# First attention of a two-block transformer kernel: the value projection spread over two query blocks, and a pair's outputs copied out of their bank by ScalarE

## The reference, cut to what matters

```python
SEQ, QBLK, ATT_HEADS, ATT_HEAD_DIM = 512, 128, 16, 64
def forgetting_attention(q, k, v, log_f):
    scale = ATT_HEAD_DIM ** -0.5
    F = jnp.transpose(jnp.cumsum(log_f, axis=1), (0, 2, 1))
    q, k, v = (jnp.transpose(t, (0, 2, 1, 3)) for t in (q, k, v))
    for blk in range(S // QBLK):
        s0, s1 = blk * QBLK, (blk + 1) * QBLK
        logits = jnp.einsum('bhqd,bhkd->bhqk', q[:, :, s0:s1], k[:, :, :s1]) * scale
        logits = logits + F[:, :, s0:s1, None] - F[:, :, None, :s1]
        mask = jnp.arange(s0, s1)[:, None] >= jnp.arange(s1)[None, :]
        p = jax.nn.softmax(jnp.where(mask, logits, -jnp.inf), axis=-1)
        outs.append(jnp.einsum('bhqk,bhkd->bhqd', p, v[:, :, :s1]))
# q, k, v are columns of h @ w_in (h: 512 x 1024); all in float32
# beside it, independent of it: silu(c_2) @ mod_mix_w_2 and silu(c_2) @ mod_ffn_w_2
```

## Time and profile before

| what | us |
|---|---|
| median of three runs | 2661.47 |
| lowest and highest run | 2659.76, 2664.95 |
| span of the profiled execution, first to last instruction | 2654.8 |
| the attention stage in it, first matmul of the stage to the first of the next | 52.2 to 307.7 |
| one pair in it (pairs 1 to 5) | 30.0 |

### The profile page before, as it was taken

One profiled execution on the slowest core, in us unless ns is written; L12 is line 12 of the kernel. 1 busy time (PEld: TensorE's weight loads), 2 busy tenths in 40 slices (PEclk: granted clock), 3 DMA queues, 4 the chain that ended last, 5 costly groups with the idle time before them and its releaser, 6 DMA issues. The chain is left out here.

```text
span 2654.8 us, 33834 instructions
## 1 busy us (share of the span) xinstructions
PE 2503.1 (94%) x13321; PEld 1989.2 (75%) x13321; DVE 1729.9 (65%) x2508; ACT 1139.0 (43%) x1641; POOL 63.4 (2%) x166
## 2 busy tenths in 40 slices
PE   7999899999989999899988899999999989999998
PEld 5666578777767877788875457888888877788886
DVE  4899545588875666899965565677766664632435
ACT  5444422255564235688853344522324253531323
POOL 0000000000000001000001000000000000000000
PEclk9999999999999988999999999999999899999999
DMA  7887727333235734999962203234332423233321
GB/s 263 264 284 270 245 82 276 91 104 95 80 104 191 257 61 167 355 420 419 417 250 92 78 27 104 80 119 135 111 111 77 127 87 121 65 107 98 95 80 32
DMA packets 299502, 427.44 MB, mean 161 GB/s; under 512 B 27690, under 2 KB 213533, under 8 KB 289488
## 3 DMA queue, kind: packets, MB, share of 16 engines
q1 hardware_dynamic: 289424, 395.13, 43.4%
q0 software_dynamic: 5392, 20.97, 2.0%
q10 hardware_dynamic: 4528, 9.18, 0.9%
HBM read 384.11 MB, written 41.14 MB: 160 GB/s over the span
## 5 line engine op out<-in xcount | busy, mean ns | idle before, releaser
L3724 PE MATMUL banks<-big,late_parts 128*128 128x512 f32 x1920 | 443.0, 393 | 5.9 <-PEq L151 3.8
L3724 PEld LDWEIGHTS banks<-big,late_parts 128*128 128x128 f32 x1920 | 363.3, 189 | 84.1 <-issue 6.1
L3724 PE MATMUL banks<-h_parts_second,late_parts 128*128 128x512 f32 x1440 | 331.1, 390 | 4.7 <-DVE h_parts_second L3936 4.7
L3724 PEld LDWEIGHTS banks<-h_parts_second,late_parts 128*128 128x128 f32 x1440 | 271.0, 188 | 61.2 <-issue 5.1
L3912 DVE TENSOR_TENSOR late_parts<-w_second,late_parts 128x2048 fp32r<-128x2048 f32 x69 | 158.1, 2292 | 218.7 <-ACT late_parts L3797 218.5
L2379 DVE TENSOR_TENSOR expert_parts<-w,expert_parts 128x2048 fp32r<-128x2048 f32 x102 | 232.7, 2288 | 21.7 <-ACT expert_parts L2375 20.8
L3797 ACT ACTIVATE late_parts<-w_second 128x2048 fp32r<-128x2048 f32 x69 | 132.0, 1914 | 255.9 <-PE banks L3724 255.9
L1344 PE MATMUL banks<-h_parts,ssm_parts 128*128 128x512 f32 x960 | 229.0, 396 | 0.8 <-DVE ssm_parts L1611 0.4
L2375 ACT ACTIVATE expert_parts<-w 128x2048 fp32r<-128x2048 f32 x102 | 194.8, 1916 | 60.6 <-PE banks L2386 54.7
L1344 PEld LDWEIGHTS banks<-h_parts,ssm_parts 128*128 128x128 f32 x960 | 178.5, 188 | 43.3 <-issue 6.4
L2386 PE MATMUL banks<-expert_parts,expert_xt 128*128 128x512 f32 x816 | 192.4, 395 | 4.0 <-DVE expert_xt L2367 4.0
(11 more groups left out here) (703 smaller groups left out, 3851.2 us busy)
## 6 DMA issues: line engine op xcount, KB each, us to landing
w_second<-in_mlp_w_dram SPq DMA_DIRECT2D x64, 1024.0 KB, 5.2
w<-in_w_exp_gate_dram SPq DMA_DIRECT2D x34, 1024.0 KB, 9.6
w<-in_w_exp_up_dram SPq DMA_DIRECT2D x34, 1024.0 KB, 9.4
w<-in_w_exp_down_dram SPq DMA_DIRECT2D x34, 1024.0 KB, 9.2
w<-in_w_in_dram SPq DMA_DIRECT2D x64, 512.0 KB, 4.6
w<-in_mod_mix_w_dram SPq DMA_DIRECT2D x24, 1024.0 KB, 5.1
w<-in_mod_ffn_w_dram SPq DMA_DIRECT2D x23, 1024.0 KB, 5.9
w<-in_w_in_dram SPq DMA_DIRECT2D x16, 1024.0 KB, 5.7
```

Source lines behind the costliest of these rows:

```text
L3724: mm = pe.matmul(ps[:, bank(n, f), :], w_part(n, w)[:, kk, f * P:(f + 1) * P], x[:, v, kk, :], start=(first_chunk(n) and kk == 0 and j == ...
```

## The change

1. Value projection. A table `PIECES` gives the pieces of each block: query in block 0 and key in block 1 as before (12 + 12 matmuls), value in four pieces of 6, two in block 2 and two in block 3.
2. `turn_values(i)` moves from block 3 of the pair before to block 0 of the pair itself, ahead of the query projection, and writes the upper halves of banks 4 and 5, not bank 7. `turn(i, 0)` now waits for its copy, `v_copied`. `copy_values(i)` on ACT stands behind `exponent(i, 1)`.
3. `sum_mod(i-1)`, `copy_rows` and `turn_mod(i-1)` move from block 0 to block 1, and the wait for `mod_copied` and `copy_mod` from block 1 to block 2, since the values now use these half banks in block 0.
4. `copy_out(i-1)` moves from DVE to ACT, behind `copy_values(i)` in block 0; for the last pair it is ACT's last instruction.
5. `evict` and `high` of the value go from block 2 to block 3 on ACT; `low(i+2, 2)` on DVE goes from block 3 of pair i to block 0 of pair i+1 (there called `low(i+1, 2)`).
6. On SP `halves.load(0)`, which waits for the last `low`, goes from ahead of the first strip of pair 6 to ahead of its fourth.

```diff
@@ -790,2 +790,3 @@
     GROUP = 32
+    PIECES = (((0, 0, 4), (0, 4, 8)), ((1, 0, 4), (1, 4, 8)), ((2, 0, 2), (2, 2, 4)), ((2, 4, 6), (2, 6, 8)))
     mod_matrices = (k.ins["mod_mix_w_2"], k.ins["mod_ffn_w_2"])
@@ -853,3 +854,3 @@
                         load_qkv(k, sp, i + 2)
-                    if i == final - 1 and j == 0:
+                    if i == final - 1 and j == MOD_SLOTS:
                         sp.wait_ge(s["w_low"], 3 * pairs)
@@ -874,5 +875,3 @@
                     pe.wait_ge(s["w_low"], 3 * i + j + 1)
-                    if i > 0 and j == 0:
-                        pe.wait_ge(s["v_copied"], i)
-                    elif i > 0:
+                    if i > 0:
                         pe.wait_ge(s["proj_copied"], 3 * i + j)
@@ -887,4 +886,7 @@
                 pe.wait_ge(s["proj_copied"], 3 * i + 3)
+                if i > 0:
+                    pe.wait_ge(s["turned_copied"], UNITS * i)
                 for b in range(TB):
-                    mm = pe.transpose(ps[:, 7, b * P:(b + 1) * P], vt[:, b * P:(b + 1) * P], k.ident[:])
+                    at = HALF + b % 2 * P
+                    mm = pe.transpose(ps[:, 4 + b // 2, at:at + P], vt[:, b * P:(b + 1) * P], k.ident[:])
                 mm.then_inc(s["v_turned"], 1)
@@ -905,4 +907,5 @@
             def turn(i, b):
-                if b == 0 and i > 0:
-                    pe.wait_ge(s["turned_copied"], UNITS * i)
+                if b == 0:
+                    pe.wait_ge(s["v_copied"], i + 1)
+                if b == 1 and i > 0:
                     sum_mod(i - 1)
@@ -918,6 +921,4 @@
             def weigh(i, b):
-                if b == 0:
-                    pe.wait_ge(s["v_copied"], i + 1)
-                    if i > 0:
-                        pe.wait_ge(s["o_copied"], i)
+                if b == 0 and i > 0:
+                    pe.wait_ge(s["o_copied"], i)
                 pe.wait_ge(s["turned_copied"], UNITS * i + 2 * b + 2)
@@ -962,3 +963,2 @@
             project(0, 2, 0, KD)
-            turn_values(0)
             pe.wait_ge(s["mask_ready"], 2)
@@ -971,8 +971,7 @@
                         scores(i + 1, 0)
+                    if b == 0:
+                        turn_values(i)
                     if i + 1 < pairs:
-                        if b < 3:
-                            project(i + 1, b, 0, KD // 2)
-                        else:
-                            turn_values(i + 1)
-                    if i > 0 and b == 1:
+                        project(i + 1, *PIECES[b][0])
+                    if i > 0 and b == 2:
                         pe.wait_ge(s["mod_copied"], i)
@@ -983,4 +982,4 @@
                     turn(i, b)
-                    if i + 1 < pairs and b < 3:
-                        project(i + 1, b, KD // 2, KD)
+                    if i + 1 < pairs:
+                        project(i + 1, *PIECES[b][1])
                     if i == final and 1 <= b < 3:
@@ -988,3 +987,3 @@
                     weigh(i, b)
-                    if i > 0 and b == 0:
+                    if i > 0 and b == 1:
                         turn_mod(i - 1)
@@ -1009,3 +1008,4 @@
                 act.wait_ge(s["v_turned"], i + 1)
-                act.activation(v[:, i % 2], ps[:, 7, :].rearrange("p (b n) -> p b n", b=TB), ACT.Copy).then_inc(s["v_copied"], 1)
+                dst = v[:, i % 2].rearrange("p (e b) n -> p e (b n)", e=2)
+                act.activation(dst, ps[:, 4:6, HALF:], ACT.Copy).then_inc(s["v_copied"], 1)
 
@@ -1043,2 +1043,6 @@
                 ins.then_inc(s["mod_copied"], 1)
+
+            def copy_out(i):
+                act.wait_ge(s["weighed"], duals * (i + 1))
+                act.activation(o[:, i, :], ps[:, 6, :], ACT.Copy).then_inc(s["o_copied"], 1)
 
@@ -1059,3 +1063,2 @@
                 high(1, j)
-            copy_values(0)
             exponent(0, 0)
@@ -1067,12 +1070,15 @@
                         exponent(i + 1, 0)
-                        copy_values(i + 1)
-                    if i > 0 and b == 1:
+                    if b == 0:
+                        copy_values(i)
+                        if i > 0:
+                            copy_out(i - 1)
+                    if i > 0 and b == 2:
                         copy_mod(i - 1)
                     copy_turned(i, b)
-                    if i > 0 and b == 0:
+                    if i > 0 and b == 1:
                         copy_rows(i - 1)
-                    if i + 1 < pairs and b < 3:
-                        evict(i + 1, b)
-                        if i + 2 < pairs:
-                            high(i + 2, b)
+                    if i + 1 < pairs and b != 2:
+                        evict(i + 1, min(b, 2))
+                    if i + 2 < pairs and b != 2:
+                        high(i + 2, min(b, 2))
                     if i == final - 1 and b == duals - 1:
@@ -1083,2 +1089,3 @@
             copy_mod(final)
+            copy_out(final)
 
@@ -1114,6 +1121,2 @@
                     dve.tensor_scalar(row, row, rinv[:, at:at + 1], None, ALU.mult).then_inc(s["probs_done"], 1)
-
-            def copy_out(i):
-                dve.wait_ge(s["weighed"], duals * (i + 1))
-                dve.tensor_copy(o[:, i, :], ps[:, 6, :]).then_inc(s["o_copied"], 1)
 
@@ -1160,5 +1163,5 @@
                     normalise(i, b)
-                    if i > 0 and b == 0:
-                        copy_out(i - 1)
-                    if i + 2 < pairs and b >= 1:
+                    if b == 0 and 1 <= i < final:
+                        low(i + 1, 2)
+                    if i + 2 < pairs and 1 <= b < 3:
                         low(i + 2, b - 1)
@@ -1168,3 +1171,2 @@
                         halves.low(dve, 0)
-            copy_out(final)
 
```

## The result

| | before | after |
|---|---|---|
| median, runs of both side by side (nine each) | 2659.76 us | 2668.16 us |
| ratio, with 95% interval | | 1.0041 (1.0031 to 1.0050) |
| span of the profiled execution | 2654.8 us | 2664.6 us |
| first matmul of the following stage (L551) | 307.68 | 315.03 |

The changed kernel is slower, by 8.4 us between the medians and by 11 us (8 to 13) by the ratio. The forecast was +5.9 us and 2667.4 us; the time lies inside the range. The interval does not hold 5.9 us, though, so the sum was too small. That the time itself is only 0.8 us from the forecast is luck: the nine runs of before have their median 1.7 us lower than the three that the forecast was added to.

What follows compares the result with a forecast made beforehand. The hand-over loop between PE and DVE in the attention stage was taken as the bound. Pair 0 +1.0, pairs 1 to 5 +4.0, pair 6 -0.7, pair 7 +1.6 gave +5.9 us: 2667.4 us, range 2661 to 2672.5.

Steps and rivals of the forecast that it cites:

- The loop of before, 30.0 us: Steady pair before: PE from T0 to R0, 21.14 us, then DVE from R0 to next T0, 8.86 us.
- The loop of after, 30.8 us: Pairs 1 to 5: PE from T3 to R3, 21.9 us, DVE from R3 to T3, 8.9; +4.0 us over five pairs.
- Signs: Steady pair's idle times: DVE before R3 about 2.2 us, R0 none; PE before T3 1.5, T2 1.2, W3 none, T0 little.
- The copy of the outputs, nothing: Block 0: moving the 0.60 us copy_out from DVE to ACT gains nothing, as DVE idles before R2 anyway.
- The wait for `mod_copied`, hidden: Block 2: PE waits 1.2 us for copy_mod before T2, hidden because DVE is later still.
- Pair 6, -0.7: Pair 6 falls from 30.39 to 29.7 us: no low in block 2, and the moved load frees the strips.
- Pair 7, +1.6: Last pair and end: net +1.4 from waits and moved work, +0.5 for the last copy_out, less 0.2 for clock.
- Pair 0, +1.0: First pair: T0 waits for the value copy until 73.8, not 72.88, delaying the next pair's S1 by 1.0 us.
- Rival 1: The fill works: R3 does not wait, pairs take 28.5 to 29.0 us, kernel about 2657 us; chance 0.07.
- Rival 2: Pairs 6 and 7 give it back: pair 7's clock stays 2.4 GHz, period 30.6, about 2663 us; chance 0.20.
- Rival 3: Clock falls in every pair behind PE's waits, some 1.5 us in each of six, +9 more, 2676 us; chance 0.07.

Runs made afterwards that it cites:

- the division of the matvec alone: Kernel before with each pair's 24 matvec instructions shared over blocks 0 to 3 as 8, 7, 4, 5, not six each: 2662.63 us, ratio 1.0017.
- first values ahead: Kernel after with the first pair's values turned by PE and copied by ACT ahead of the loop: 2666.07 us, ratio 1.0031.
- copy_mod early: Kernel after with copy_mod on ACT at the head of block 2, ahead of exponent of block 3: 2667.16 us, ratio 1.0036.
- shares 6, 6, 8, 4: Kernel after with a pair's 24 matvec instructions divided 6, 6, 8, 4 over blocks 0 to 3, not six each: 2685.17 us, one execution.
- no spreading: Kernel after with all 24 value matmuls, evict and high of the value back in block 2, other edits kept: 2670.85 us, ratio 1.0043.
- shares 8, 7, 4, 5: Kernel after with a pair's 24 matvec instructions divided 8, 7, 4, 5 over blocks 0 to 3, not six each: 2658.29 us, ratio 1.0005.
- the fill and the shares fitted to it: Kernel after with matvec shares 8, 7, 3, 6, copy_mod and value copy earlier, first pair's values ahead, last copy_out on DVE: 2647.24 us, ratio 0.9970.

## Why the prediction was right, and where it was not

- **The loop of before, 30.0 us.** Its length was right, but it was half of the picture: a second one, PE's work with its two waits, is as long. The prediction read those two waits as slack under the first loop. For the forecast it made no difference, since the change lengthens the first; for someone who wants a faster kernel it is the point, as the division of the matvec alone showed.
- **The loop of after, 30.8 us.** Right: 30.84 to 30.86, made up of 21.90 and 8.92 where the sum had 21.9 and 8.9. The two taken terms, 0.9 for T3 and 0.45 for the turning of the values, were good together; pairs 1 to 5 gave +4.2 for +4.0. Two matvec more in block 2 made the pair 1.58 us longer, which is exactly theirs; two less took off 1.36, and then PE's own work with its wait for `mod_copied` came last.
- **Signs.** R3 idle 2.33 (announced 2.2), none before R0, none before W3, T0 none. Before T2 1.02 for 1.2, before T3 1.22 for 1.5.
- **The copy of the outputs, nothing.** Right in the pair, twice. In the last pair, where the copy stands last on ACT, PE's wait at the barrier is 0.49 us longer with it, as the sum had it; the other 1.6 us of the 2.1 are a stretch of low clock ahead of the copy.
- **The wait for `mod_copied`, hidden.** Right in the pairs of after, not once the shares are mended: there it is the one wait left. In the last pair it was counted at 2.6 and took 2.35.
- **Pair 6, -0.7.** Right: -0.69, no wait for a DMA. The load back in its place shows why.
- **Pair 7, +1.6.** Measured +1.0 to L551, and near by errors that partly cancelled. The sum took `sum_mod` (0.99) as new in this pair, but it stood there before too, in block 0 at 282.05; without it the term is 0.6. PE's waits grew by 1.6 us where the sum had 1.2: 2.09 ahead of T0 for 1.47, 2.35 for 1.90, 1.07 for 0.58 at the barrier. PE's busy time fell by 0.5 (22.90 to 22.41). In the kernel with `copy_out` on DVE, whose waits but the last are the same, it is 20.84 us, by the clock alone; so this pair's time is only good to 1.6 us.
- **Pair 0, +1.0.** This term was mis-sized: +2.8 at S1 of pair 1 (the pair is 4.2 longer, but starts 1.4 earlier, since the turning of the first values has left its old place, where it took 0.59 us and a wait of 0.69). The step that failed is "T0 now starts after exponent of block 1 and the value copy: 72.66 + 0.48 + 0.65 = 73.8, not 72.88", and behind it "The delay goes through: +1.0". T0's time was near (74.10), but the price was taken as the shift of T0 alone. PE's idle time ahead of T0 became 4.40 us where it was 2.20: T0 came 1.2 us later, and PE reached the gap 1.0 us earlier. Behind it the clock stayed low for longer. Before and after, from 72 to 80 us:

```profile
72.00:80.00 8.00, 7.12 (x29) 5.11 (x30) 6.01 (x17) 3.43 (x11) 0.00 (x0) 0.79 1.00 304
72.00:80.00 8.00, 5.90 (x18) 4.32 (x18) 5.52 (x15) 2.64 (x12) 0.00 (x0) 0.57 0.93 287
```

PE's busy time over the pair, the same work, was 28.53 us before (66.80 to 99.08) and 29.89 after, so the clock took 1.4 us more, most of the 1.8 that the term lacks. The working had a gap of twice the length in it and left the clock out, though for pair 7 it asked about the clock. The kernel with the first values ahead gave back 1.55 us of the 2.8.
- **What was missing: the start of the next stage.** The sum ended at the barrier. After it the granted clock was 0.89 over 15 us instead of 1.00, +1.6 us. Ahead of it PE had waited 0.74 and 1.07 us. In after the low stretch is the first 4 us of the stage (0.57). It is there in five of the eight kernels that have these two waits (after itself, copy_mod early, first values ahead, shares 6, 6, 8, 4, no spreading) and not in the other three (shares 8, 7, 4, 5; the load back; the kernel before with `copy_out` on ACT). Where the last copy is on DVE, the waits are 0.74 and 0.58 and it never came. The last copy on ACT is thus not enough for it; what else decides was not settled.
- **The total.** 7.35 us to L551 and 1.6 behind it make 9.0 of the 9.8 by which the spans differ. The forecast had +5.9; pair 0's 1.8 and the next stage's 1.6 are most of what it lacks, pair 7 has 0.6 less than its term, and about 0.9 is in the later stages.

Rival 1 was wrong for this kernel, and right about what the new order can hold: with the fill and the shares fitted to it, the pair falls to 29.0. The Trainium skill (Perfetto Trace Analysis, Identifying the Most-Contended Engine) would have it that the engine with the highest occupancy is to be worked on first; here 27.28 us of DVE's work and 28.5 of PE's make pairs of 30.85, 29.49 and 29.00 us, by order alone, and 0.6 us taken off DVE made no pair shorter by more than 0.02 us. No run took work off PE. Rival 2, that the end gives it back, did not come: the clock of pair 7 was 0.88 and its waits grew. Rival 3 did not come in after; it came in the kernel with two matvec more in block 2, and in two pairs of the one without the spreading.

What stays open is a part of the time that no stage shows. With `copy_out` on ACT in the kernel before, the stage ended 0.5 us earlier, the span was 1.6 us longer, and by the ratio the kernel took 5 us more (3 to 8). From the start of the following stage to the last instruction all twelve kernels have the same code, and their traces take 2346.7 to 2353.9 us for it (before 2347.1, after 2349.6), with stretches of low clock that fall at other moments from kernel to kernel. So a few us of the total cannot be laid to a stage by adding up its gain alone; I did not find the cause.

## What to carry to other kernels

Where two engines that work in order are both nearly full, follow the work around the loop that they form: from a hand-over on one engine to the next on the other and back, and add it up. A move of work is worth what it does to the longest such loop, not to an engine's busy time; a filler put into one engine's gap lengthens every loop that passes it, so shift the other engine's filler (here two of the six 0.78 us instructions of block 2) out of the same half with it. And look at the first and the last turn of a loop apart, the clock included: here pair 0, pair 7 and the start of the next stage hold 5.4 of the 9.8 us between the two spans, and 3.0 of it, in pair 0 and the next stage, is more time at the low clock behind PE's waits.

## What the runs showed of the chip

- The same idle time of PE was followed by a fall of the clock in one pair or kernel and not in the next. With 1.02 and 1.22 us a pair (after) the granted clock stayed at 1.00 (2.4 GHz) in pairs 1 to 5. With 1.27 and 0.74 us (no spreading) it did so in four pairs and fell in the next two (0.96 and 0.91 over the pair). With 2.8 us before T3 it fell in four of five steady pairs, to 0.95 and 1.5 us each. Behind 2.35 us in the last pair it fell in after and not in the kernel with `copy_out` on DVE. Behind 4.40 us in pair 0 it was 0.57 over 72 to 80 us, behind 2.20 us 0.79.
- One DMA issue held on SP by a semaphore cost DVE 7.95 us of waiting for strips that were queued behind it and did not depend on it.
- Off the loop an instruction's place was free: copy_out of 128x512 costs 0.60 us on ACT or DVE, and moving it changed a pair by 0.02 us.
